# A streaming encoder layer on 8 cores: the running stream last, the residual added by an accumulating DMA, and weights that arrive in smaller pieces

## The chip, the cores and the metric

The kernel runs on the 8 NeuronCores of one Trainium2 chip. Each core computes one prompt stream of 2048 frames and two running streams of 16 frames; the cores exchange nothing. The metric is the device time in microseconds (us) of the slowest core.

## What is computed

```python
def _layer(x, pos, S_ret, S_hg, w_in, w_out, g_pre, g_post, lb):
    h = _rmsnorm(x, g_pre)
    u = jnp.einsum('btd,de->bte', h, w_in)
    cuts = np.cumsum([RET_WIDTH] * 4 + [HG_WIDTH] * 3)
    rq, rk, rv, rg, hq, hf, hi, hg = jnp.split(u, cuts.tolist(), axis=-1)
    ...
    hq = jax.nn.silu(_heads(hq, HG_HEADS))
    f = lb + (1.0 - lb) * jax.nn.sigmoid(_heads(hf, HG_HEADS))  # forget gate in (lb, 1)
    logf = jnp.log(f)
    hk = 1.0 - f
    hv = _heads(hi, HG_HEADS)
    o_r, o_h, S_ret, S_hg = _run_mixers(S_ret, S_hg, rq, rk, rv, hq, hk, hv, logf, log_gamma)
    o = jnp.concatenate([jax.nn.silu(rg) * _merge(_head_norm(o_r)), jax.nn.silu(hg) * _merge(_head_norm(o_h))], axis=-1)
    y = jnp.einsum('bte,ed->btd', o, w_out)
    return x + _rmsnorm(y, g_post), S_ret, S_hg
```

The model width is 1024; w_in is 1024 x 4096 and its columns are 8 segments of 512 (0 and 1: the retention's q and k; 2 and 3: its v and gate; 4 and 5: HGRN2's q and forget gate; 6 and 7: its v and gate). w_out is 1024 x 1024. Both recurrences have 4 heads of 128 and carry one 128 x 128 state per head. All inputs are fp32.

## The kernel before

A core's prompt is cut into 4 blocks of 512 frames, and each block into 4 tiles of 128 frames. Its two running streams are one more block, called the sample, with one tile of 48 rows. Every step is recorded once by `S.op(engine, function, reads, writes)`; afterwards `Sched.list_schedule` simulates the engines with a table of costs and writes the order of each engine out. That order is fixed in the program: each engine (PE, ACT, DVE, POOL, and SP, which only issues DMAs) works through its list and waits at an operation until its inputs are there. `add_fillers` puts small matmuls of the identity (L1047) into places where the simulation sees PE idle.

- `front(block)` runs `stage_A` for each tile: load x into `xs` (the first two odd ones into `xr`), sum of squares on ACT, power on POOL, scaling into `xbf` on DVE (L619), transposed into `xT` by PE in block 0 and the sample (L633) and by a transposing DMA elsewhere (L625). It then runs `stage_B_hg` for each head: two projections of the whole block (L654, segments 5 and 4), ACT, two scans on DVE, products on POOL (L721, L731).
- `tile(block, j)` runs `stage_B_ret` (segments 0 and 1, L671, rotary products on DVE, sums on POOL in L759, transposes), `stage_C` (segments 2, 6, 3, 7, L671), `stage_D` (scores L835, output L867 and L872, state update L884, head norms: ACT L895, POOL L899 and L902, DVE L905) and `stage_E`.
- `stage_E` transposes the gated output `og` into `ogT` (by DMA at L926, or by PE at L934 in block 0, in the sample and in the last tile), multiplies by `Wo` (two banks of 8 matmuls, L947), sums the squares on ACT (L951), multiplies the bank by `gpost` on DVE (L954), takes the power on POOL (L957, L959), and on DVE scales and adds x (L962). That x was loaded a second time into `xr` by SP (L923). SP stores `xr` to `yp` (L970). There are two `xr` buffers.

The weights are fp32 in HBM and bf16 in SBUF, so POOL issues their DMAs, which cast. Segments 0 and 1 (the first pair) come in four pieces of 2 x 128 rows, the other pairs and `Wo` in two pieces of 4 x 128 rows. Only the projections of segments 0 and 1 in block 0 are split into four groups of two matmuls, so that each group waits for its piece alone. A projection holds one of the 8 PSUM banks from its first matmul on, and `RESP` = 3 banks are kept free of projections when one is placed. In `front` and `tile` the program order is: blocks 0 to 2; block 3 with tiles 0 to 2; the sample; tile 3 of block 3.

## Time and profile before

| | |
|---|---|
| time, median of 3 runs | 387.5 us (386.18 to 388.3) |
| the profiled execution | 388.32 us, span of its slowest core 386.8 us |
| spans of the 8 cores in it | 381.1 to 386.8 us |
| PE, DVE, POOL, ACT busy | 93%, 66%, 53%, 47% of the span |

The span runs from the first to the last instruction of a core. The profiled execution took 1.5 us more than its slowest span. A matmul is pipelined: its busy time in a row holds some 0.16 us that the next one overlaps, so the step between the starts of two matmuls in a row tells more than the duration of one. Times in the rows are from the start of the span.

### The profile page before, as it was taken

The page shows a single profiled execution, that of the slowest core. Times are in us where ns is not written, and L with a number is a line of the kernel's source. Part 1 is how long each engine was busy: PE and PEld are TensorE (multiplying, and loading weights), DVE is VectorE, ACT ScalarE, POOL GpSimd, SP SyncE. Part 2 cuts the span into 40 slices and gives each one's busy share as a digit, 9 for nine tenths or more (in the row PEclk, how much of TensorE's full clock was granted, in tenths as well). Part 3 has the DMA queues.
Part 4 walks back from the last instruction along what each step waited for, and adds up shares of the span by engine and source line. Part 5 has one row for each costly group of instructions (what it writes and reads, how often), then busy time and mean ns, then how long its engine had stood idle before and what let it go on. Part 6 is the DMA issues. An engine that isn't in the chain of part 4 may idle for free.

```text
span 386.8 us, 8100 instructions; the slowest of 8 cores (381.1 to 386.8 us)
## 1 busy us (share of the span) xinstructions
PE 358.8 (93%) x2339; PEld 188.1 (49%) x2339; DVE 255.6 (66%) x554; ACT 180.9 (47%) x563; POOL 205.5 (53%) x277
## 2 busy tenths in 40 slices
PE   8599799998988989997999999999999999999982
PEld 8554354455544444453545454545455554554541
DVE  0316565827889998969395949386849467486364
ACT  2431245557767546471636253446262533646341
POOL 8525541545775785774283645375837436347130
PEclk9989899999999999998999999999999999999988
DMA  7999999996488476964537335432233443233217
GB/s 177 204 177 165 202 163 168 178 242 150 87 219 173 157 169 146 231 160 102 153 67 190 88 121 73 164 71 64 55 125 72 133 107 97 110 56 79 101 22 225
DMA packets 64700, 52.62 MB, mean 136 GB/s; under 512 B 45840, under 2 KB 53040, under 8 KB 64656
## 3 DMA queue, kind: packets, MB, share of 16 engines
q1 hardware_dynamic: 59344, 41.61, 42.4%
q0 software_dynamic: 5312, 10.49, 17.7%
q8 instruction: 20, 0.33, 0.4%
q14 instruction: 24, 0.20, 0.2%
HBM read 41.73 MB, written 10.09 MB: 134 GB/s over the span
## 4 chain that ended last, share of the span: by engine, by line
PE 78%; DVE 6%; DMA 5%; issue 3%; POOL 3%; ACT 2%; SPq 1%; DVEq 0%; ACTq 0%; POOLq 0%; another core or an unknown queue 0%
PE bank L671 42%; PE bank L947 14%; PE bank L654 12%; DMA xr<-xp 4%; PE bank L867 2%; PE bank L835 2%; DVE xbf L619 2%; PE bank L872 2%; PE bank L884 2%; POOL QTh L731 1%; DVE fG L713 1%; DVE fR L725 1%; PE bank L934 1%; DMA ogT<-og 1%; SPq L849 1%
## 5 line engine op out<-in xcount | busy, mean ns | idle before, releaser
L671 PE MATMUL bank<-Wi,xT 128*128 128x512 bf16 (+1 forms) x816 | 187.8, 382 | 0.7 <-DVE Sst L889 0.7
L671 PEld LDWEIGHTS bank<-Wi,xT 128*128 128x128 bf16 (+1 forms) x816 | 78.3, 99 | 88.1 <-issue 4.1
L947 PE MATMUL bank<-Wo,ogT 128*128 128x512 bf16 (+1 forms) x272 | 65.1, 391 | 3.6 <-DMA ogT<-og 2.0
L905 DVE SCALAR_TENSOR_TENSOR og<-bank,rsq,gate 128x128 bf16<-128x128 f32 (+1 forms) x136 | 38.6, 343 | 41.2 <-POOL rsq L902 18.3
L654 PE MATMUL bank<-xT,Wi 128*128 128x512 bf16 (+1 forms) x320 | 63.0, 342 | 2.1 <-POOL QTh L731 0.9
L654 PEld LDWEIGHTS bank<-xT,Wi 128*128 128x128 bf16 x320 | 26.9, 98 | 34.2 <-issue 6.9
L947 PEld LDWEIGHTS bank<-Wo,ogT 128*128 128x128 bf16 (+1 forms) x272 | 26.5, 100 | 34.7 <-issue 7.4
L824 POOL TENSOR_TENSOR Sst<-Sst,decS 128x512 f32<-128x512 f32 x30 | 32.9, 1105 | 16.5 <-DVE Sst L889 8.7
L895 ACT ACTIVATE og<-bank 128x128 bf16<-128x128 f32 (+1 forms) x136 | 35.4, 291 | 9.7 <-PE bank L867 6.2
L902 POOL TENSOR_TENSOR rsq<-ssq,mhalf 128x4 f32<-128x4 f32 (+1 forms) x34 | 35.4, 1042 | 5.2 <-POOL ssq L899 0.4
L828 ACT ACTIVATE Sb<-Sst 128x512 bf16<-128x512 f32 x30 | 19.0, 634 | 38.7 <-POOL Sst L824 21.3
L759 POOL TENSOR_TENSOR qtm<-tA,tB 128x512 bf16<-128x512 f32 (+1 forms) x17 | 21.6, 1270 | 25.2 <-DVE tB L750 24.2
L951 ACT ACTIVATE og<-bank 128x512 bf16<-128x512 f32 (+1 forms) x34 | 20.4, 601 | 30.4 <-PE bank L947 25.3
L731 POOL TENSOR_TENSOR QTh<-fQ,fR 128x512 bf16<-128x512 f32 (+1 forms) x20 | 23.0, 1151 | 21.4 <-ACT fQ L729 10.7
L721 POOL TENSOR_TENSOR KTh<-fG 128x512 bf16<-128x512 f32 (+1 forms) x20 | 18.5, 924 | 28.0 <-DVE fG L713 28.0
L794 ACT ACTIVATE gate<-bank 128x512 bf16<-128x512 f32 (+1 forms) x34 | 20.4, 600 | 27.5 <-PE bank L671 26.2
L713 DVE TENSOR_TENSOR_SCAN fG<-bank,zer 128x128 f32<-128x128 f32 (+1 forms) x72 | 23.1, 377 | 14.9 <-ACT bank L708 14.8
L895 ACT ACTIVATION_READ_ACCUMULATOR og<-bank 128x1 f32 (+1 forms) x136 | 30.4, 224 | 0.0
L619 DVE SCALAR_TENSOR_TENSOR xbf<-xs,rsx,gpre 128x1024 bf16<-128x1024 f32 (+1 forms) x15 | 21.9, 1472 | 11.8 <-POOL rsx L616 11.6
L725 DVE TENSOR_TENSOR_SCAN fR<-bank,inv,zer 128x128 f32<-128x128 f32 (+1 forms) x72 | 27.5, 439 | 2.8 <-DVE inv L717 1.1
L962 DVE SCALAR_TENSOR_TENSOR xr<-bank,rs,xr 128x512 f32<-128x512 f32 (+1 forms) x34 | 25.3, 744 | 5.8 <-POOL ssq L899 3.3
L843 DVE TENSOR_TENSOR AT<-bank,maskT 128x512 bf16<-128x512 f32 x32 | 20.9, 682 | 10.5 <-PE bank L835 10.4
(93 smaller groups left out, 450.8 us busy)
## 6 DMA issues: line engine op xcount, KB each, us to landing
xr<-xp SPq DMA_DIRECT2D x18, 512.0 KB, 4.3
yp<-xr SPq DMA_DIRECT2D x16, 512.0 KB, 2.9
xs<-xp SPq DMA_DIRECT2D x14, 512.0 KB, 5.5
Wi<-w_in POOLq DMA_DIRECT2D x6, 1024.0 KB, 48.5
Wi<-w_in POOLq DMA_DIRECT2D x4, 512.0 KB, 20.3
Wo<-w_out POOLq DMA_DIRECT2D x2, 1024.0 KB, 71.8
rot<-rot_p SPq DMA_DIRECT2D x16, 96.0 KB, 5.0
gpre<-g_pre SPq DMA_DIRECT2D x1, 512.0 KB, 6.7
```

What stands on the lines that cost most here:

```text
L619: S.op(DVE, lambda e: e.scalar_tensor_tensor(out=xbf[slot][0:L, :], in0=xbuf[0:L, :], scalar=rsx[0:L, sq:sq + 1], in1=gpre[0:L, :], op0=AL ...
L654: ins = e.matmul(pb(v)[:, 0:nt], lhsT=Wi[:, kc, col0:col0 + 128], rhs=k.xT[:, kc, 0:nt], start=(kc == 0), stop=(kc == 7))
L671: ins = e.matmul(pb(v)[0:L, :], lhsT=k.xT[:, kc, j * 128:j * 128 + L], rhs=Wi[:, kc, seg * 512:(seg + 1) * 512], start=(kc == 0), stop=(kc ...
L713: S.op(DVE, lambda e, c=c: e.tensor_tensor_scan(out=G[:, c, rsl(cl - 1, cl)], data0=pb(v)[:, rsl(c * st_ + cl - 1, cl)], data1=zer[:, 0:cl ...
L725: S.op(DVE, lambda e, c=c: e.tensor_tensor_scan(out=pack(R)[:, c, :], data0=pb(v)[:, c * st_:c * st_ + cl], data1=zer[:, 0:cl], initial=IV ...
L731: S.op(POOL, lambda e: e.tensor_tensor(out=tok(k.QT[:, h, :]), in0=pack(SQ), in1=pack(R), op=ALU.mult), reads=["fQ", ("fR", f)] + [("fR", ...
L824: S.op(POOL, lambda e, Sst=Sst, cc=cc, g=g, gsl=gsl: e.tensor_tensor(out=Sst[:, gsl].rearrange("p (h e) -> p h e", h=4), in0=Sst[:, gsl].r ...
L895: S.op(ACT, lambda e, q_=q_, h=h, vo=vo: e.activation(out=ogs[vs][0:L, h * 128:(h + 1) * 128], in_=pb(vo)[0:L, q_ * 128:(q_ + 1) * 128], f ...
L902: S.op(POOL, lambda e, gq=gq, g=g: e.tensor_tensor(out=rsq[vs][0:L, gq], in0=ssq[vs][0:L, gq], in1=mhalf[0:L, 0:4], op=ALU.pow), reads=[(" ...
L905: S.op(DVE, lambda e, q_=q_, h=h, vo=vo: e.scalar_tensor_tensor(out=ogs[vs][0:L, h * 128:(h + 1) * 128], in0=pb(vo)[0:L, q_ * 128:(q_ + 1) ...
L947: ins = e.matmul(pb(y)[0:L, :], lhsT=ogT[:, kc, 0:L], rhs=Wo[:, kc, n * 512:(n + 1) * 512], start=(kc == 0), stop=(kc == 7))
L962: S.op(DVE, lambda e, n=n: e.scalar_tensor_tensor(out=xr[slot][0:L, n * 512:(n + 1) * 512], in0=pb(ybk[n])[0:L, :], scalar=rs2[0:L, 0:1], ...
```

## The change

- The second pair of segments is also loaded in four pieces, and in block 0 every projection is now split: in four groups for the first two pairs, in two groups for the others (`PARTS`), for `proj_fm` too.
- `stage_E` of 15 prompt tiles no longer loads x ahead and no longer multiplies by `gpost` apart. DVE multiplies bank, scale and `gpost` in one operation into `xr`; then POOL issues a DMA that adds x from HBM onto `xr` in SBUF, and SP stores `xr` when that has landed. The last tile of block 3 and the sample keep the old form.
- All weight DMAs have priorities one above the other; the x loads of tiles 4 and 5 wait for the third pair's last piece (was: the fourth pair's), and the load of `gpost` waits for the fourth pair's last piece (was: the first scores).
- The sample comes behind tile 3 of block 3.
- The simulation's model of the DMA queues is new, and its priorities get a fixed small noise, so the order changes in many places all over the program.

```diff
-DMA_RATE = 300.0
-SW_RATE = 275.0
-HW_SHARED = 120.0
+DMA_RATE = 310.0
+DMA_RATE_0 = 230.0
+HW_SHARE = 0.45
...
+class Net:
+    def __init__(self):
+        self.t = 0.0
+        self.queues = ([], [])
+        self.coming = []
+
+    def issue(self, t, soft, nbytes, op):
+        self.coming.append([max(t, self.t), 0 if soft else 1, float(nbytes), op])
+        self.coming.sort(key=lambda x: x[0])
...
+            rate = DMA_RATE if self.t > 12000.0 else DMA_RATE_0
+            rates = [rate] if len(on) == 1 else [rate * (1.0 - HW_SHARE), rate * HW_SHARE]
...
-                if e == POOL:
-                    if o["nbytes"] > 600000:
-                        sw_free = max(fin, sw_free) + o["nbytes"] / SW_RATE
-                        dlat = (sw_free - fin) + o["lat"]
-                    else:
-                        dlat = 4500.0
-                else:
-                    share = 9000.0 < fin < sw_free
-                    hw_free = max(fin, hw_free) + o["nbytes"] / (HW_SHARED if share else DMA_RATE if o["lat"] > 1500.0 else 150.0)
-                    dlat = (hw_free - fin) + o["lat"] + (3000.0 if share else 0.0)
-                o["t_land"] = fin + dlat
-                o["t_dma"] = o["nbytes"]
+                net.issue(fin + (4500.0 if e == POOL else 0.0), e == POOL, o["nbytes"], i)
+                if e != POOL and o["nbytes"] < 120000 and len(net.queues[0]) > 1:
+                    o["lat"] += 3500.0
...
-        loads = [(w_in_v, Wi, "Wi", 0, 2), (w_in_v, Wi, "Wi", 1024, 4), (w_in_v, Wi, "Wi", 2048, 4), (w_in_v, Wi, "Wi", 3072, 4),
+        loads = [(w_in_v, Wi, "Wi", 0, 2), (w_in_v, Wi, "Wi", 1024, 2), (w_in_v, Wi, "Wi", 2048, 4), (w_in_v, Wi, "Wi", 3072, 4),
...
-                S.ops[wid]["boost"] = (14.0e6 if wb < 4 else 10.0e6) - 5e5 * wb
+                S.ops[wid]["boost"] = 14.0e6 - 4e5 * wb
...
                 elif i < 6:
-                    S.ops[xid]["deps"].add(S.last_w[("Wi", 7, 3)])
+                    S.ops[xid]["deps"].add(S.last_w[('Wi', 5, 3)])
...
+        PARTS = (4, 4, 2, 2)
...
-            S.op(PE, mm, reads=WK(seg) + [("xT", k.par, j) for j in range(k.ns)], writes=[v] + claim)
+            parts = PARTS[seg // 2] if (not k.sample and k.b == 0) else 1
+            for q in range(parts):
+                k0, k1 = q * 8 // parts, (q + 1) * 8 // parts
+
+                def mm(e, k0=k0, k1=k1):
+                    ins = None
+                    for kc in range(k0, k1):
+                        ins = e.matmul(pb(v)[:, 0:nt], lhsT=Wi[:, kc, col0:col0 + 128], rhs=k.xT[:, kc, 0:nt],
+                                       start=(kc == 0), stop=(kc == 7))
+                    return ins
+                S.op(PE, mm, reads=WK(seg, k0 // 2, k1 // 2) + [("xT", k.par, j) for j in range(k.ns)], writes=[v] + (claim if q == 0 else []))
...
-            parts = 4 if (not k.sample and k.b == 0 and seg < 2) else 1
+            parts = PARTS[seg // 2] if (not k.sample and k.b == 0) else 1
...
                     for did in late_dma:
-                        S.ops[did]["deps"].add(scid)
+                        S.ops[did]["deps"].add(S.last_w[("Wi", 7, 3)])
...
+            acc = not k.sample and not (k.b == 3 and j == 3)
...
-            else:
+            elif not acc:
...
-                S.op(DVE, lambda e, n=n, y=y: e.tensor_tensor(out=pb(y)[0:L, :], in0=pb(y)[0:L, :],
-                                                              in1=gpost[0:L, n * 512:(n + 1) * 512], op=ALU.mult),
-                     reads=[y, "gpost", ("ss2", n)], writes=[y])
+                if not acc:
+                    S.op(DVE, lambda e, n=n, y=y: e.tensor_tensor(out=pb(y)[0:L, :], in0=pb(y)[0:L, :],
+                                                                  in1=gpost[0:L, n * 512:(n + 1) * 512], op=ALU.mult),
+                         reads=[y, "gpost", ("ss2", n)], writes=[y])
             S.op(POOL, lambda e: e.tensor_scalar(out=rs2[0:L, :], in0=ss2[0:L, 0:1], scalar1=ss2[0:L, 1:2], scalar2=EPS,
                                                 op0=ALU.add, op1=ALU.add), reads=[("ss2", 0), ("ss2", 1)], writes=["rs2"])
             S.op(POOL, lambda e: e.tensor_tensor(out=rs2[0:L, :], in0=rs2[0:L, :], in1=mhalf[0:L, 0:1], op=ALU.pow),
                  reads=["rs2", "mhalf"], writes=["rs2"])
-            for n in range(2):
-                S.op(DVE, lambda e, n=n: e.scalar_tensor_tensor(out=xr[slot][0:L, n * 512:(n + 1) * 512], in0=pb(ybk[n])[0:L, :],
-                                                                scalar=rs2[0:L, 0:1], in1=xr[slot][0:L, n * 512:(n + 1) * 512],
-                                                                op0=ALU.mult, op1=ALU.add),
-                     reads=[ybk[n], "rs2", ("xr", slot)], writes=[("xr", slot)])
+            if acc:
+                for n in range(2):
+                    S.op(DVE, lambda e, n=n: e.scalar_tensor_tensor(out=xr[slot][0:L, n * 512:(n + 1) * 512], in0=pb(ybk[n])[0:L, :],
+                                                                    scalar=rs2[0:L, 0:1], in1=gpost[0:L, n * 512:(n + 1) * 512],
+                                                                    op0=ALU.mult, op1=ALU.mult),
+                         reads=[ybk[n], "rs2", "gpost"], writes=[("xr", slot) if n == 0 else ("xr1", slot)])
+                S.op(POOL, lambda e: e.dma_start(out=xr[slot][:], in_=xp[t0:t0 + 128, :], accum_op=ALU.add),
+                     reads=[("xr1", slot)], writes=[("xr", slot)], dma_key=("xacc", slot))
...
-                stores.append(S.op(SP, lambda e: e.dma_start(out=yp[t0:t0 + 128, :], in_=xr[slot][:]), reads=[("xr", slot)], dma_key=("st", slot)))
+                stores.append(S.op(SP, lambda e: e.dma_start(out=yp[t0:t0 + 128, :], in_=xr[slot][:]), reads=[("xr", slot), ("xr1", slot)], dma_key=("st", slot)))
...
             if b == 3:
-                for j in range(3):
+                for j in range(4):
+                    if j == 4:
+                        front(smp)
+                        tile(smp, 0)
                     tile(blocks[b], j)
-                front(smp)
-                tile(smp, 0)
-                tile(blocks[b], 3)
+                if 4 == 4:
+                    front(smp)
+                    tile(smp, 0)
...
+        S.jitter = (15, 500.0)
```

PE, the stretch in which block 0 goes from segments 0 and 1 to segments 2 and 3. L671 (L733 in the changed kernel) is a projection with `Wi`, L774 (L836) the transposes of rotated q and k, L835 (L897) the scores of a tile, L1047 a filler. Before:

```order
16 L774 MATMUL bank<-ident,qtm 128x128 x4
17 L774 MATMUL bank<-ident,Ktr 128x128 x4
18 L671 MATMUL bank<-Wi,xT 128x512 x6
19 L835 MATMUL bank<-QKr 128x128 x4
20 L671 MATMUL bank<-Wi,xT 128x512 x6
21 L774 MATMUL bank<-ident,qtm 128x128 x4
22 L774 MATMUL bank<-ident,Ktr 128x128 x4
23 L1047 MATMUL bank<-ident 128x128 x12
24 L774 MATMUL bank<-ident,qtm 128x128 x4
25 L774 MATMUL bank<-ident,Ktr 128x128 x4
26 L1047 MATMUL bank<-ident 128x128 x6
27 L671 MATMUL bank<-Wi,xT 128x512 x16
```

The changed kernel, the same place:

```order
10 L733 MATMUL bank<-Wi,xT 128x512 x40
11 L836 MATMUL bank<-ident,qtm 128x128 x4
12 L836 MATMUL bank<-ident,Ktr 128x128 x4
13 L733 MATMUL bank<-Wi,xT 128x512 x4
14 L897 MATMUL bank<-QKr 128x128 x4
15 L733 MATMUL bank<-Wi,xT 128x512 x4
16 L836 MATMUL bank<-ident,qtm 128x128 x4
17 L836 MATMUL bank<-ident,Ktr 128x128 x4
18 L733 MATMUL bank<-Wi,xT 128x512 x22
19 L836 MATMUL bank<-ident,qtm 128x128 x4
20 L836 MATMUL bank<-ident,Ktr 128x128 x4
21 L733 MATMUL bank<-Wi,xT 128x512 x6
```

Projections stand now where fillers stood, and between the transposes of the tiles there are 22 and more of them.

SP, the first part of the program, behind the loads of the first tiles. Before:

```order
9 L984 DMA rot<-rot_p 128x192 x3
10 L560 DMA gpost<-g_post 128x1024
11 L984 DMA rot<-rot_p 128x192 x2
12 L602 DMA xs<-xp 128x1024 x2
13 L923 DMA xr<-xp 128x1024 x2
14 L625 DMA_TRANSPOSE xT<-xbf 128x8x128
15 L602 DMA xs<-xp 128x1024
16 L625 DMA_TRANSPOSE xT<-xbf 128x8x128
17 L602 DMA xs<-xp 128x1024
```

The changed kernel:

```order
9 L1058 DMA rot<-rot_p 128x192 x5
10 L658 DMA xs<-xp 128x1024 x3
11 L681 DMA_TRANSPOSE xT<-xbf 128x8x128 x2
12 L658 DMA xs<-xp 128x1024
13 L616 DMA gpost<-g_post 128x1024
14 L681 DMA_TRANSPOSE xT<-xbf 128x8x128
15 L658 DMA xs<-xp 128x1024
16 L681 DMA_TRANSPOSE xT<-xbf 128x8x128
17 L658 DMA xs<-xp 128x1024
18 L1058 DMA rot<-rot_p 128x192
```

The loads and transposes of block 1's tiles stand ahead of `gpost`, and the loads of `xr` are gone from the queue.

PE, the end of the program. L867 and L872 are the output of a tile's heads, L884 (L946) the state updates, L934 (L998) the transposes of `og`, L947 (L1011) the product with `Wo`; operands of 48 or 16 belong to the sample. Before:

```order
469 L872 MATMUL bank<-Sb,QTh 128x128
470 L947 MATMUL bank<-Wo,ogT 48x512 x16
471 L857 MATMUL bank<-ident,KTh 48x128 x4
472 L884 MATMUL bank<-V,Ktr 128x128 x12
473 L934 MATMUL bank<-ident,og 128x128 x8
474 L884 MATMUL bank<-V,Kth 128x128 x8
475 L947 MATMUL bank<-Wo,ogT 128x512 x16
476 L884 MATMUL bank<-V,Kth 128x128 x4
```

The changed kernel:

```order
475 L934 MATMUL bank<-xbf,QTh 16x128 x2
476 L1011 MATMUL bank<-Wo,ogT 128x512 x16
477 L919 MATMUL bank<-ident,KTh 48x128 x4
478 L946 MATMUL bank<-V,Ktr 128x128 x8
479 L998 MATMUL bank<-ident,og 128x48 x8
480 L946 MATMUL bank<-V,Kth 128x128 x4
481 L1011 MATMUL bank<-Wo,ogT 48x512 x16
```

The sample's output product is last instead of the prompt's, and the prompt tile's stands behind the sample's last heads.

## Rows read from the trace of the kernel before

**Rows 1.** Cores: us from first to last instruction, granted TensorE clock.
```profile
core 7: 386.8 us, clock 0.980
```

**Rows 2.** Windows of core 7: us busy (instructions) of each engine, clock, DMA share, GB/s.
```profile
20.00:40.00 20.00, 19.35 (x132) 10.65 (x130) 9.39 (x24) 3.99 (x6) 6.93 (x8) 0.92 1.09 172
40.00:60.00 20.00, 17.66 (x118) 9.35 (x118) 10.66 (x22) 7.32 (x23) 9.43 (x10) 0.91 1.08 182
...
90.00:110.00 20.00, 18.13 (x132) 9.99 (x132) 16.88 (x30) 14.64 (x50) 13.95 (x20) 1.00 0.60 131
...
130.00:150.00 20.00, 18.82 (x105) 8.94 (x104) 18.29 (x33) 10.69 (x35) 14.36 (x17) 1.00 0.60 157
...
200.00:340.00 140.00, 139.43 (x844) 70.79 (x842) 96.19 (x215) 63.67 (x225) 74.89 (x98) 1.00 0.39 104
```

**Rows 3.** The chain of work that ended last, shares of the span by engine.
```profile
PE 78%; DVE 6%; DMA 5%; issue 3%; POOL 3%; ACT 2%; SPq 1%; DVEq 0%; ACTq 0%; POOLq 0%; another core or an unknown queue 0%
```

**Rows 4.** Timeline of PE: start, us, line, operation, count, idle before.
```profile
39.51 0.50 PE L1047 MATMUL bank<-ident 128*128 128x128 bf16 x6
...
43.43 5.30 PE L671 MATMUL bank<-Wi,xT 128*128 128x512 bf16 x16
...
59.79 5.34 PE L654 MATMUL bank<-xT,Wi 128*128 128x512 bf16 x24 [0.19 <-DMA Wi<-w_in]
...
92.25 3.62 PE L947 MATMUL bank<-Wo,ogT 128*128 128x512 bf16 x16
```

**Rows 5.** Weight DMAs on POOL: duration, first and last issue; time to landing.
```profile
L543 POOL DMA_DIRECT2D Wi<-w_in x2: 748/774/800, 4.4 to 5.1; - x2
DMA to landing us min/median/max: 24.8/28.0/31.2
...
L543 POOL DMA_DIRECT2D Wi<-w_in x2: 792/797/802, 5.8 to 6.5; - x2
DMA to landing us min/median/max: 37.1/41.6/46.1
...
L543 POOL DMA_DIRECT2D Wi<-w_in x1: 826/826/826, 8.8 to 8.8; - x1
DMA to landing us min/median/max: 50.9/50.9/50.9
...
L543 POOL DMA_DIRECT2D Wi<-w_in x2: 760/765/770, 9.6 to 10.3; - x2
DMA to landing us min/median/max: 56.3/58.9/61.6
...
L543 POOL DMA_DIRECT2D Wo<-w_out x2: 760/795/830, 12.9 to 13.7; - x2
DMA to landing us min/median/max: 66.5/71.8/77.1
```

**Rows 6.** Groups by line and form: count, busy us, mean ns, idle before.
```profile
L954 DVE TENSOR_TENSOR bank<-bank,gpost 128x512 f32<-128x512 f32 x32 | 21.8, 689 | 3.9 <-ACT og L951 3.9
```

**Rows 7.** DMA issues: count, KB each, median us from issue to landing.
```profile
xr<-xp SPq DMA_DIRECT2D x18, 512.0 KB, 4.3
yp<-xr SPq DMA_DIRECT2D x16, 512.0 KB, 2.9
```

**Rows 8.** Two loads at the start, under the weights' traffic.
```profile
xr<-xp SPq DMA_DIRECT2D x2, 512.0 KB, 14.2
```

**Rows 9.** Waits of PE from 90 to 180 us: total, times, longest.
```profile
PE bank L934 <- DVE og L905: 2.3, 3, 1.2
PE bank L947 <- DMA ogT<-og: 2.0, 1, 2.0
PE bank L835 <- POOL QTh L731: 0.9, 1, 0.9
```

**Rows 10.** Timeline of SP's queue and of PE around 172 us.
```profile
172.80 1.22 SPq L926 DMA_TRANSPOSE ogT<-og  x1
176.10 3.01 PE L947 MATMUL bank<-Wo,ogT 128*128 128x512 bf16 x8 [2.00 <-DMA ogT<-og]
```

**Rows 11.** Timeline of the last tile: PE, then SP's last store.
```profile
374.16 5.30 PE L947 MATMUL bank<-Wo,ogT 128*128 128x512 bf16 x16 [1.04 <-ACT ogT L937]
...
383.38 0.34 SPq L970 DMA_DIRECT2D yp<-xr  x1
```

More of the change, by code:

```diff
@@ L175, in list_schedule @@
             prio[i] += o.get("boost", 0.0)
+        if self.jitter is not None:
+            noise = np.random.RandomState(self.jitter[0]).uniform(-1.0, 1.0, n) * self.jitter[1]
+            for i in range(n):
+                prio[i] += float(noise[i])
         XLAT = 110.0
@@ L186, in list_schedule @@
                 avail[o["eng"]].append(i)
-        free_t = {e: 0.0 for e in ENGS}
-        sw_free, hw_free, cold = 11500.0, 0.0, 0.0
-        port_free = 0.0
+        free_t = {e: 900.0 for e in ENGS}
+        cold, port_free = 0.0, 0.0
+        net = Net()
         order = {e: [] for e in ENGS}
@@ L197, in free_bank, with landed @@
             return min(fr, key=lambda k: (free_at[k], k))
+        def landed(until):
+            out = net.advance(until)
+            for i, t in out:
+                o = ops[i]
+                t += o["lat"]
+                o["t_land"] = t
+                for sx in succ[i]:
+                    ready_t[sx] = max(ready_t[sx], t + XLAT)
+                    ndeps[sx] -= 1
+                    if ndeps[sx] == 0:
+                        avail[ops[sx]["eng"]].append(sx)
+            return len(out)
         while done < n:
@@ L227, in list_schedule @@
                     best = (e, cand[1], cand[2])
+            if landed(best[2] if best is not None else None):
+                continue
             if best is None:
@@ L280, in list_schedule @@
                     avail[ops[sx]["eng"]].append(sx)
-        self.est_makespan = max(free_t.values())
+        landed(1e9)
+        self.est_makespan = max(max(free_t.values()), max(o.get("t_land", 0.0) for o in ops))
         return order
```

53 lines of the change are left out of this document (43 added, 10 removed).

## The prediction

> **What bounds the kernel now.** I read the cores first: the slowest span is 386.8 us [rows 1]; the execution took 388.3 us, 1.5 more, and lies 0.8 above the median of the runs (387.5). Then the chain of work that ended last: PE holds 78% of it, no other engine over 6% [rows 3]. So the time is PE's work plus the places where PE doesn't get on. The windows say where those are [rows 2]. From 200 to 340 us PE is busy for 139.43 of 140 us at clock 1.00: there a freed engine buys nothing. The losses lie before, and in the last tile.
>
> PE's work can be priced by the step: 16 full-width matmuls take 3.62 us, and 0.16 of it overlaps the next, so 0.216 each; a 128-column one takes (0.50 - 0.16) / 6 = 0.056 [rows 4]. In the first 90 us PE is fed by the weight stream, with the DMA engines full (share 1.09 and 1.08 [rows 2]). Issue plus time to landing [rows 5]: the first pair is complete at 4.4 + 24.8 = 29.2 us, the second has its halves at 36.3 and 42.9, the third at 52.6 and 59.7, the fourth at 65.9 and 71.9, `Wo` at 79.4 and 90.8. PE has finished segments 0 and 1 by 39.5, plays fillers and waits, and begins segments 2 and 3 at 43.43, right behind the landing at 42.9. Those 16 matmuls take 5.30 us instead of 3.62: the granted clock fell during the wait (mean 0.91 of 2.4 GHz over that window, some of it at the 1.2 GHz level) [rows 2, 4]. At 59.79 PE again starts on a landing; `Wo` lands at 90.8 and is first used at 92.25 [rows 4].
>
> **The change, step by step: pieces and splits.** I counted in each kernel's PE order how much work stands ahead of the wait for each landing, and took it off the landing time. The result is how late PE would run, at the least, for that wait alone; the largest so far rules. Before: second pair 64 full and 60 small matmuls, 17.2 us of work, 42.9 - 17.2 = 25.7; third 120 and 100, 31.5, so 28.2; fourth 184 and 104, 45.5, so 26.4; `Wo` 240 and 156, 60.5, so 30.3. The real start at 92.25 gives 31.8: 1.5 of other waits on top.
>
> Changed, with the same landings: last piece of the second pair 82 and 60, 21.1 us, so 21.8; third pair, first half 104 and 88, 27.4, so 25.2, second half 134 and 100, 34.5, so 25.2; fourth, first half 176 and 104, 43.8, so 22.1, second half 200 and 108, 49.2, so 22.7; `Wo` 300 and 156, 73.5, so 17.3. The wait for `Wo` goes, since 60 more full-width matmuls, block 1's among them, stand ahead of it. What is late next is the third pair (25.2) and then perhaps the fourth, because the x loads now start when the third pair has landed. A 2 MB half piece landed 6.0 us behind the one before it (65.9 to 71.9), so two x loads of 0.5 MB cost some 3 us of stream and four cost 6: the fourth pair's 22.7 becomes 25.7 or 28.7. `gpost`, 0.5 MB, leaves the third pair's stretch and gives it 1.5 us. I take 25.7. Against 31.8 that is 6.1 us, and I leave the 1.5 us of other waits as they are: **-4.6 us**. Bounds: 0 (all given back at block 1's transposes) and -6.6 - 1.5 = -8.1 (25.2, no other waits).
>
> **DVE and the order of blocks 0 to 2.** 30 multiplications by `gpost` go: 0.689 us each [rows 6], 20.7 us of DVE. The operation that takes their place is of the same form as the scaling-and-adding that it replaces, so nothing is added. From 200 us on it's hidden by PE's own work. From 90 to 180 DVE is 84 to 91% busy in the two windows shown [rows 2] and PE waits: 2.3 us for `og` from DVE, 2.0 for `ogT`, 0.9 for `QTh`, and 2.4 in smaller ones not shown; the 8 matmuls behind the `ogT` wait then take 3.01 us instead of 8 x 0.216 + 0.16 = 1.89, and as much again is lost right after [rows 9, 10]. That is 7.6 us of waits and some 1.7 of slow clock. About 8 of the 30 multiplications fall in this stretch, 5.5 us. The new order will have waits of its own, so I take somewhat under half: **-4 us** (bounds 0 and -9).
>
> **The tail.** Before, the last tile is a prompt tile, and after its heads' output PE has too little to do: it waits 1.04 us for the last `ogT`, 0.6 for `og` ahead of that, and its last 16 matmuls take 5.30 us, 1.7 above 3.62 [rows 11]: 3.4 us in all. Now the prompt tile's product with `Wo`, 3.45 us, lies in the gap in which the sample's last heads are normed. The norm (four squares on ACT, power on POOL, four products on DVE, transposes, copy) takes some 4.5 us and PE has 4.3 us of work for it. What follows the last matmul is the same chain with 48 rows and two small stores in place of one. **-2 us** (bounds 0 and -3.4).
>
> **The accumulating DMA.** No row shows one. Its bytes are those of the `xr` load that it replaces, so the traffic stays. What changes is that it stands between DVE's last operation on a tile and the store, and the store stands in SP's in-order queue with the transposes for `QKr`, `Kth` and `ogT` behind it. Below, it takes what the plain load took, 4.3 us; above, what such a load took under full traffic, 14.2 [rows 7, 8]. I take 6, nearer to the plain one, since most of these come after the weights. The new order's simulation allows 4.5 + 2.0 + 0.5 MB / 310 KB per us = 8.2 us, so at 6 SP hardly waits at the store. An `xr` buffer then is taken for 6 + 2.9 us more, and its tile comes round only two tiles later, some 40 us. POOL issues 15 more DMAs at some 0.8 us [rows 5], 12 us over a span in which it is 53% busy; behind one of them stand head norms of the next tile, hidden by PE's backlog from 200 us on. **+1 us** for both (bounds 0 and +12: three or four stalls like the one at 172.80, of 2.0 us and the slow clock behind it).
> The Trainium skill ("DMA: Bandwidth & Descriptors", on the anatomy of a DMA issued by GpSimd) gives such a DMA 2.0 us + bytes / 436 KB per us, an estimated 3.2 us for 0.5 MB; it prices no addition, and by it the sum wouldn't move.
>
> **The sum.** 388.3 - 4.6 - 4 - 2 + 1 = 378.7 for an execution like the profiled one, and 377.9 against the median: 378.
>
> **Rivals.**
> (a) The lead is given back in block 0: four x loads and block 1's transposing DMAs go into the full stream, the fourth pair and `Wo` land 6 us later, and projections of block 1 wait for `xT`, whose last transposes stand behind `gpost` in SP's queue. For it: DMA share 1.08 then. Against it: `Wo` has 13 us to spare. Only 1 of the 4.6 us stays: 382. Chance 0.18.
> The same page of the Trainium skill (on issuing engines not being separate DMA queues) says that DMAs of all engines run on the same 16 DMA engines and interleave; the share near 1 agrees, and it speaks for this case.
> (b) Slower: the accumulating DMA takes over some 9 us, so SP stands at the store past its planned time and the transposes behind it come late for PE, tile after tile. At 12 us, 4 late each time, with about 4 to spare at most places, 1 to 2 us in ten tiles and a fall of the clock in a few: +14 in place of +1, 391. It decides from about 9 us on. For it: 14.2 us under traffic, and one late `ogT` cost nearly 4 us at 172.80. Against it: 4.3 us is the usual. Chance 0.13.
> (c) The waits from 90 to 180 go nearly all, and the tail's: 372.5. For it: DVE has 5 us less to do there. Chance 0.13.
> (d) Gains and new waits cancel, or the accumulate's added waits just match the lead: 387. Chance 0.06.
> My forecast has 0.50, with its own range of 375 to 381.5.
>
> **Range and chances.** Over 0.5% of 387.5, about 2 us, is what a measurement of this kernel can tell. Faster: 0.50 + 0.18 + 0.13 = 0.81, less a little for (a) coming out worse, 0.80. Within 0.5%: 0.07. Slower: 0.13. The range goes from 371.5, (c) with a margin, to 387, which holds (a) and leaves (b) out.
>
> **What would show it.** In the profile after: no fillers and no gap ahead of segments 2 and 3, and granted clock 1.00 from 40 to 60 us; the first product with `Wo` some 13 us of work further on in PE's order, at 99 to 101 us; DVE busy some 235 us; PE still full from 200 to 340; the last `Wo` product at full clock. The accumulate's time from issue to landing decides (b): near 6 us I'm right on it. I'd be wrong if PE waited for transposing DMAs more than 2 or 3 us in all, if the fourth pair landed after 76 us, or if new waits of DVE and POOL in blocks 0 and 1 ate the lead.

## The result: 2.2% slower

The changed kernel takes **396.9 us** (median of four executions, 395.99 to 410.74) against 387.9 for the kernel before, run beside it: a ratio of **1.022 [1.017, 1.028]**. Predicted were 378.0 us and a range of 371.5 to 387, so it is a miss by 18.9 us, on the other side of no change. In some executions of these kernels one die ran at a lower clock; they are left out of every ratio and time below.

The page of the profiled execution (396.8 us; core 6, span 395.2). The chain of work that ended last, by engine and by line:

```profile
PE 70%; DMA 12%; DVE 6%; issue 4%; POOL 4%; ACT 3%; POOLq 0%; DVEq 0%; ACTq 0%; SPq 0%
PE bank L733 39%; PE bank L1011 12%; PE bank L716 11%; DMA xT<-xbf 7%; DMA Wi<-w_in 5%; PE bank L929 2%; PE bank L934 2%; PE bank L946 2%; PE bank L897 2%; DVE tA L808 1%; DVE fG L775 1%; DVE AT L905 1%; DVE xbf L675 1%; ACT og L1015 1%; DVE fR L787 1%
```

PE had 78% of it before [rows 3]; DMA has gone from 5 to 12%, and 7% of the span are the transposing DMAs into `xT`, which the page before doesn't show among its largest rows. The windows of core 6 say where:

```profile
40.00:60.00 20.00, 19.59 (x124) 10.07 (x126) 10.83 (x22) 7.40 (x23) 9.43 (x10) 1.00 1.07 169
...
80.00:90.00 10.00, 3.35 (x16) 1.32 (x14) 0.00 (x0) 0.89 (x1) 0.00 (x0) 0.90 1.27 169
90.00:110.00 20.00, 17.11 (x102) 9.48 (x105) 13.76 (x21) 12.98 (x37) 12.61 (x16) 0.80 0.45 115
130.00:150.00 20.00, 19.03 (x106) 9.25 (x106) 13.97 (x30) 11.25 (x29) 15.62 (x19) 1.00 0.70 157
...
170.00:200.00 30.00, 25.66 (x132) 12.33 (x133) 20.35 (x44) 11.70 (x35) 17.95 (x20) 0.89 0.57 104
200.00:340.00 140.00, 138.91 (x835) 71.28 (x848) 90.31 (x200) 66.10 (x234) 84.82 (x107) 1.00 0.52 107
```

From 40 to 60 us it is as predicted: PE full, clock 1.00 where it was 0.91 [rows 2]. Then, from 80 to 90, DVE and POOL do nothing and PE is busy for 3.35 us, after which the granted clock is 0.80 on the mean over 20 us (PE runs partly at 1.2 GHz). A second, smaller loss lies from 170 to 200. From 200 to 340 nothing has changed. PE's two longest waits from 60 to 200 us (total, times, longest):

```profile
PE bank L897 <- POOL QTh L793: 9.4, 1, 9.4
PE bank L929 <- DVE AT L905: 4.2, 1, 4.2
```

**How late PE runs.** For a point in PE's order I take its start and subtract the priced work ahead of it (0.216 us a full-width matmul, 0.056 a 128-column one, as in the prediction; fillers count nothing). A step in this number is a loss, wherever it is waited for. Worked out from the starts of each profiled execution's slowest core (e4 and e5 are described below; the x gate is the weight piece that block 1's first two x loads wait for; 328 is the start of the last product with `Wo`):

```
us of work ahead     20    35    50    55    65    80   130   140   328
before             27.7  28.0  29.4  29.8  31.4  33.7  36.6  41.5  46.1
changed            23.6  24.2  31.0  43.2  43.3  44.0  53.0  53.1  56.2
x gate back (e5)   22.0  22.8  25.3  26.1  29.5  36.2  42.1  42.3  45.4
before + pieces    24.6  25.9  32.4  32.6  33.4  34.1  38.0  40.1  44.7
```

The changed kernel is 4.1 us ahead at 20 us of work and has lost that at 50. It loses 12.2 at one place between 50 and 55, and 7.0 at another just before 130 (170 us of the span), where the kernel before has a loss of 4.9 of its own a little later. From 140 to 328 it gains 1.5, and 1.7 more inside the last product, which took 5.30 us before [rows 11] and takes 3.61 now. That leaves 10.1 - 1.7 = 8.4 us, the difference of the two spans. The gate's row shows that e5 isn't free of loss either: between 55 and 80 it loses 10.1 us, where the changed kernel loses 0.8. What the gate is worth below is what is left of both.

### The profile page after: what moved, and what is told of

Its sections match the earlier page's. It is cut to its first block, busy times and chain, and to the rows that moved or that the text cites. A ratio compares the mean times of both kernels' runs of the same rounds, so it can differ in the third digit from the quotient of the medians.

```text
span 395.2 us, 7895 instructions; the slowest of 8 cores (388.8 to 395.2 us)
## 1 busy us (share of the span) xinstructions
PE 357.1 (90%) x2303; PEld 188.5 (48%) x2341; DVE 237.4 (60%) x524; ACT 181.1 (46%) x563; POOL 223.0 (56%) x294
## 4 chain that ended last, share of the span: by engine, by line
PE 70%; DMA 12%; DVE 6%; issue 4%; POOL 4%; ACT 3%; POOLq 0%; DVEq 0%; ACTq 0%; SPq 0%
PE bank L733 39%; PE bank L1011 12%; PE bank L716 11%; DMA xT<-xbf 7%; DMA Wi<-w_in 5%; PE bank L929 2%; PE bank L934 2%; PE bank L946 2%; PE bank L897 2%; DVE tA L808 1%; DVE fG L775 1%; DVE AT L905 1%; DVE xbf L675 1%; ACT og L1015 1%; DVE fR L787 1%
## 5 line engine op out<-in xcount | busy, mean ns | idle before, releaser
L733 PE MATMUL bank<-Wi,xT 128*128 128x512 bf16 (+1 forms) x796 | 190.8, 387 | 4.3 <-DMA Wi<-w_in 2.3
L733 PEld LDWEIGHTS bank<-Wi,xT 128*128 128x128 bf16 (+1 forms) x816 | 79.2, 100 | 92.7 <-issue 11.7
L716 PE MATMUL bank<-xT,Wi 128*128 128x512 bf16 (+1 forms) x312 | 61.0, 339 | 3.1 <-DVE fG L775 1.4
L1011 PE MATMUL bank<-Wo,ogT 128*128 128x512 bf16 (+1 forms) x262 | 61.3, 379 | 1.5 <-ACT og L957 0.9
L957 ACT ACTIVATE og<-bank 128x128 bf16<-128x128 f32 (+1 forms) x136 | 35.7, 283 | 12.5 <-PE bank L934 8.7
L886 POOL TENSOR_TENSOR Sst<-Sst,decS 128x512 f32<-128x512 f32 x30 | 31.3, 1050 | 17.7 <-DVE Sst L951 9.8
L1011 PEld LDWEIGHTS bank<-Wo,ogT 128*128 128x128 bf16 (+1 forms) x272 | 26.0, 98 | 30.0 <-issue 0.8
L821 POOL TENSOR_TENSOR qtm<-tA,tB 128x512 bf16<-128x512 f32 (+1 forms) x17 | 23.5, 1382 | 17.0 <-DVE tB L812 13.7
L890 ACT ACTIVATE Sb<-Sst 128x512 bf16<-128x512 f32 x30 | 19.0, 632 | 29.7 <-POOL Sst L886 18.4
L787 DVE TENSOR_TENSOR_SCAN fR<-bank,inv,zer 128x128 f32<-128x128 f32 (+1 forms) x72 | 28.2, 440 | 2.5 <-DVE inv L779 0.9
L957 ACT ACTIVATION_READ_ACCUMULATOR og<-bank 128x1 f32 (+1 forms) x136 | 29.2, 214 | 0.0
L951 DVE TENSOR_TENSOR Sst<-bank,Sst 128x512 f32<-128x512 f32 x30 | 20.1, 685 | 14.3 <-PE bank L946 11.3
L812 DVE TENSOR_TENSOR tB<-bank,rot 128x512 f32<-128x512 f32 (+1 forms) x34 | 22.9, 682 | 8.7 <-PE bank L733 6.7
```

Source lines behind the costliest of these rows:

```text
L716: ins = e.matmul(pb(v)[:, 0:nt], lhsT=Wi[:, kc, col0:col0 + 128], rhs=k.xT[:, kc, 0:nt], start=(kc == 0), stop=(kc == 7))
L733: ins = e.matmul(pb(v)[0:L, :], lhsT=k.xT[:, kc, j * 128:j * 128 + L], rhs=Wi[:, kc, seg * 512:(seg + 1) * 512], start=(kc == 0), stop=(kc ...
L787: S.op(DVE, lambda e, c=c: e.tensor_tensor_scan(out=pack(R)[:, c, :], data0=pb(v)[:, c * st_:c * st_ + cl], data1=zer[:, 0:cl], initial=IV ...
L821: S.op(POOL, lambda e, ts=ts, dst=dst: e.tensor_tensor(out=dst[0:L, :], in0=tA[ts][0:L, :], in1=tB[ts][0:L, :], op=ALU.add), reads=[("tA", ...
L886: S.op(POOL, lambda e, Sst=Sst, cc=cc, g=g, gsl=gsl: e.tensor_tensor(out=Sst[:, gsl].rearrange("p (h e) -> p h e", h=4), in0=Sst[:, gsl].r ...
L957: S.op(ACT, lambda e, q_=q_, h=h, vo=vo: e.activation(out=ogs[vs][0:L, h * 128:(h + 1) * 128], in_=pb(vo)[0:L, q_ * 128:(q_ + 1) * 128], f ...
```

## The stop at 80 to 93 us, row by row

SP's queue in the changed kernel, then who waited on core 6: ACT, POOL, DVE, PE (start, us, ..., idle time before and its releaser).

```profile
71.90 13.26 SPq L681 DMA_TRANSPOSE xT<-xbf  x2
85.32 0.47 SPq L658 DMA_DIRECT2D xs<-xp  x1
...
93.80 1.25 SPq L681 DMA_TRANSPOSE xT<-xbf  x1
```
```profile
89.11 1.06 ACT L666 ACTIVATE xbf<-xs 128x1024 bf16<-128x1024 f32 x1 [11.52 <-DMA xT<-xbf]
...
90.65 0.59 ACT L791 ACTIVATE fQ<-bank 128x512 f32<-128x512 f32 x1
...
91.38 1.26 POOL L793 TENSOR_TENSOR QTh<-fQ,fR 128x512 bf16<-128x512 f32 x1
...
91.47 2.25 DVE L675 SCALAR_TENSOR_TENSOR xbf<-xs,rsx,gpre 128x1024 bf16<-128x1024 f32 x1 [12.11 <-POOL rsx L672]
...
92.79 0.58 PE L897 MATMUL bank<-QTh,KTh 128*128 128x128 bf16 x4 [9.44 <-POOL QTh L793]
```

And the two transposing DMAs of 71.9 and 75.7 us: duration on the queue (min/median/max, ns) and time to landing.

```profile
L681 SPq DMA_TRANSPOSE xT<-xbf x2: 3516/6476/9437, 71.9 to 75.7; - x2
...
DMA to landing us min/median/max: 13.8/15.4/17.1
```

The first transposing DMA of block 1 goes out at 71.90, since its x load no longer waits for the fourth pair, and lands 17.07 us later (71.90 to 88.97). The same operation of the kernel before goes out at 89.6 and later, as the last weights land (90.8 [rows 5]):

```profile
L625 SPq DMA_TRANSPOSE xT<-xbf x6: 1217/1222/1332, 89.6 to 122.1; - x6
...
DMA to landing us min/median/max: 3.1/3.2/3.4
```

ACT's next operation is the sum of squares of the next tile (L666), which writes its squares into the same `xbf` buffer that the transposing DMA still reads. ACT works in order, so `fQ` of the heads' chain, whose projection PE had ended by 81 us, stands behind it, then POOL's `QTh`, then PE's scores. PE never waits for `xT` itself: it waits for block 0, because block 1's preparation stands ahead of it in ACT's queue.

The early gate costs time before the stop, too. The two x loads go out at 57.9 us, in the full stream, and land after 9.0 and 11.6; ACT reaches the first sum of squares before its x is there, and a head's `decS` and the next head's operations stand behind it:

```profile
67.04 1.06 ACT L666 ACTIVATE xbf<-xs 128x1024 bf16<-128x1024 f32 x1 [3.02 <-DMA xs<-xp]
```

From 35 to 50 us of work the changed kernel loses 6.8 us and e5 2.5. I take part of the difference to be this wait; no run isolates it.

## Experiments

"Orders kept" means that every engine's order is that of the parent kernel, with only the named instructions moved or gone; "made anew" that the scheduler placed everything again. Ratios are to the kernel before, run beside each, with 95% intervals; percentages below are differences of these ratios. e1, e2 and e8 have one execution each that counts, so no ratio: their differences are in us to the changed kernel's 396.9.

```
                                      us      ratio
e3  changed, no accumulating DMAs     390.9   1.006 [1.003, 1.010]
e4  before + pieces and splits        387.7   1.000 [0.997, 1.003]
e5  changed, x gate back              387.2   0.997 [0.995, 0.999]
e6  before + accumulating stage       394.2   1.018 [1.015, 1.021]
e7  before + sample last              389.0   1.004 [1.001, 1.007]
e9  e5 with plain residual load       392.8   1.013 [1.010, 1.016]
e10 changed, plain residual load      401.8   1.034 [1.030, 1.038]
e11 e6's orders, DMAs left out        391.7   1.010 [1.006, 1.014]
e12 before + pieces + sample last     388.3   1.001 [0.999, 1.004]
e13 e5, seed 16                       389.7   1.006 [1.003, 1.009]
e14 e5, seed 17                       403.0   1.040 [1.033, 1.046]
e15 e9, seed 16                       391.8   1.010 [1.003, 1.017]
e16 e9, seed 17                       395.8   1.021 [1.016, 1.026]
e17 changed, seed 16                  399.0   1.029 [1.024, 1.034]
e18 e6, store planned later           391.8   1.011 [1.008, 1.014]
```

**e1: is it `Wo`'s traffic?** Orders kept; the two `Wo` DMAs issued on POOL behind block 0's last `KTh`.

```
+            wo = [i for i in order[POOL] if ops[i]["dma_key"] is not None and ops[i]["dma_key"][0] == "Wo"]
...
+            order[POOL] = rest[:n_] + wo + rest[n_:]
```

> The changed kernel with every engine's order kept, except that POOL issues the two w_out DMAs behind the last KTh of block 0 (77.5 us in the changed kernel's trace) instead of at 10.9 and 12.7 us. Theory T (the transposing DMAs of block 1's first x tiles are slow because they share the 16 DMA engines with the weight stream, and ACT, DVE, POOL and PE stand behind their xbf buffer): they land within 4 to 8 us instead of 17.1 and 13.8, the 9.4 us wait of PE before 92.8 us is gone or under 3 us, and the time falls by 8 to 11 us to 386 to 389. Rival R1 (they are slow for a reason of their own, such as the queue of SP or the many x loads ahead): they still take over 12 us and the time stays at 396 to 397. Rival R2 (the accumulating DMAs cost the time): 396 to 397.

393.3 us, 3.6 below the changed kernel, less than I expected (386 to 389). The wait of 9.4 us is gone: with `Wo` out of the way, the two transposing DMAs at 70.9 and 74.8 us land in 5.0 and 3.1. But `Wo` is now issued at 77.5 and lands 12.5 and 18.4 us later, and the next two meet it. The third and the fourth transposing DMA of e1, core 0, each with its time to landing:

```profile
L685 SPq DMA_TRANSPOSE xT<-xbf x1: 1876/1876/1876, 81.6 to 81.6; - x1
...
DMA to landing us min/median/max: 15.6/15.6/15.6
...
L685 SPq DMA_TRANSPOSE xT<-xbf x1: 7357/7357/7357, 86.9 to 86.9; - x1
...
DMA to landing us min/median/max: 12.4/12.4/12.4
```

PE waits 5.2 us for `xT` itself now. The stall followed the weight stream: the same transposing DMAs land fast without `Wo`'s traffic and the next ones slowly with it.

**e2: is it the shared buffer?** Orders kept; more `xbf` buffers, so that the sum of squares of tiles 6 and 7 waits for no transposing DMA.

```
+                return 10 + i, xr[i % 2][:, 0:512].bitcast(BF16)
+            b = (i - 4) % 3 if i < 6 else (i - 8) % 3
+            return b, (xbf[0], xbf[1], xbx)[b]
```

> The changed kernel with every engine's order kept and more buffers for the scaled x tiles (xbf): tiles 6 and 7 use the still idle xr buffers, the later ones rotate over three. Nothing waits any more for a transposing DMA to have read its buffer, except three tiles later. Theory T: the transposes of tiles 4 and 5 remain slow (over 12 us), but ACT's sum of squares of tile 6 starts before 80 us, the wait of PE at 83 to 92.8 us shrinks to at most 3 us (xT is needed some 7 us later in PE's order), the event at 170 us (4.2 us, behind a transpose of 8.7 us) goes too, and the time falls by 8 to 14 us to 383 to 389. Rival R2 (accumulating DMAs): 396 to 397. A rival to T in which the slow transposes hold PE through xT itself and not through the buffer: PE waits as long, now at its first projection of block 1, and the time is over 393.

388.7 us, 8.1 below, within the range that I expected (383 to 389), but not by the way expected: PE's wait was to shrink to 3 us at most. SP's queue in e2, core 0, and PE's longest wait:

```profile
70.22 13.42 SPq L700 DMA_TRANSPOSE xT<-xbf  x2
83.80 0.47 SPq L676 DMA_DIRECT2D xs<-xp  x1
```
```profile
PE bank L949 <- ACT Sb L910: 7.5, 1, 7.5
```

The transposing DMAs are as slow as before, and hold SP for 13.4 us; the x load behind them is late, and ACT's sum of squares now waits for that. The stop is 7.5 us and comes later in PE's order. So the shared buffer is one link of the chain and not the whole of it: SP's queue carries the delay as well. By the measure of how late PE runs, e2 (core 0) still loses 11.3 us from 50 to 65 us of work, the changed kernel 12.3; but from 80 to 130 it loses 2.1 in place of 9.0, and about that on each of the four cores whose clock wasn't lowered. Most of what more buffers gain is gained at the second loss.

**e3: is it the accumulating DMA?** Orders kept, the 15 accumulating DMAs left out.

```
+            gone = {i for i, o in enumerate(ops) if o["dma_key"] is not None and o["dma_key"][0] == "xacc"}
...
+            order[POOL] = [i for i in order[POOL] if i not in gone]
```

> The changed kernel with every engine's order kept, without its 15 accumulating DMAs: x is not added to the output of 15 tiles, and SP stores a tile as soon as DVE has scaled it. Theory T: the 12 us at 83 to 93 us stay, since no accumulating DMA is issued before 120 us; the event at 170 us may shrink with the traffic; 393 to 397. Rival R2: SP stood at its stores for 22 us in all behind these DMAs and made transposes late for PE; then the time falls to 388 or below.

390.9 us, 6 less than the changed kernel; I had expected less from it. PE's wait for `QTh` stays, 9.2 us against 9.4, so it isn't the accumulate's. What goes is the second loss. At 151.95 us of the changed kernel an accumulating DMA (9.5 us to landing), an x load and a transposing DMA (8.7 us to landing) run together, and ACT waits again at the sum of squares:

```profile
153.68 3.29 SPq L681 DMA_TRANSPOSE xT<-xbf  x1
```
```profile
162.51 1.06 ACT L666 ACTIVATE xbf<-xs 128x1024 bf16<-128x1024 f32 x1 [5.95 <-DMA xT<-xbf]
```

PE's 4.2 us for `AT` at 170 us and the clock of 0.89 behind it follow. Without the DMAs PE loses 4.7 us from 80 to 130 us of work (e3, core 3) in place of 9.0.

**e8: both, e1 and e3.**

> The changed kernel, every order kept, with both edits of the earlier runs: w_out's DMAs issued behind the last KTh of block 0, and no accumulating DMAs (x is not added for 15 tiles). If the two causes are separate, their gains add: the late w_out gave 3 to 4 us (393.3 against 396.9), leaving the accumulates out gave 6 (390.4), so 386 to 388. If both act on the same waits, it is no better than 390.

387.8 us, as expected: 9.1 below the changed kernel, where e1 and e3 alone give 3.6 and 6. As far as one execution can tell, the two losses are separate and add up in one fixed order. PE still waits 5.0 us for `xT` here, as in e1.

**e5: the gate of the x loads, alone.** Order made anew.

```
-                    S.ops[xid]["deps"].add(S.last_w[('Wi', 5, 3)])
+                    S.ops[xid]["deps"].add(S.last_w[('Wi', 7, 3)])
```

> The changed kernel with one dependency as it was: the x loads of tiles 4 and 5 wait for the fourth pair's last weight piece again; the order is made anew with it. Theory T (transposing DMAs of block 1 beside the weight stream cost 7 to 12 us, whatever waits for them): with x loads at 74 us their transposes run behind or at the end of the w_out transfer, PE's idle time before 95 us falls from some 15 us to under 6, and the time falls by 6 to 11 us to 386 to 391, unless the first transposes still meet w_out (then 391 to 394). Rival (the wait belongs to the order and comes back in another form): 395 to 398.

387.2 us: one number in the source, with the order that follows from it, is worth **9.6 us**. Core 0's window and its transposing DMAs up to 105 us:

```profile
80.00:90.00 10.00, 7.55 (x70) 4.63 (x69) 7.30 (x16) 8.10 (x27) 8.42 (x10) 1.00 0.97 204
...
170.00:200.00 30.00, 30.00 (x182) 15.31 (x181) 21.14 (x49) 15.93 (x51) 19.31 (x25) 1.00 0.73 118
```
```profile
L681 SPq DMA_TRANSPOSE xT<-xbf x5: 1245/1727/2788, 82.4 to 104.3; - x5
...
DMA to landing us min/median/max: 3.6/4.6/8.4
```

The first goes out at 82.4 us in place of 71.9, with less of `Wo` left to land. In all seven profiled kernels with the early gate (the changed one, e1, e2, e3, e8, e10, e17) the slowest of these DMAs issued from 60 to 105 us takes 15.4 to 17.5 us to land; in those with the late gate it takes 3.2 to 5.1 (the old scheduler) and 8.1 to 11.3 (the new).

**e4, e7, e12: the parts in the kernel before,** its scheduler kept, order made anew.

```
-        loads = [(w_in_v, Wi, "Wi", 0, 2), (w_in_v, Wi, "Wi", 1024, 4), (w_in_v, Wi, "Wi", 2048, 4), (w_in_v, Wi, "Wi", 3072, 4),
+        loads = [(w_in_v, Wi, "Wi", 0, 2), (w_in_v, Wi, "Wi", 1024, 2), (w_in_v, Wi, "Wi", 2048, 4), (w_in_v, Wi, "Wi", 3072, 4),
...
-                for j in range(3):
+                for j in range(4):
```

> The kernel before, its own scheduler and DMA priorities, with the second weight pair in four pieces and the projections of block 0 split by PARTS, and nothing else of the change; the order is made anew. My prediction's step on pieces: PE goes on through 39 to 43 us without a wait and at full clock, a gain of 3 to 5 us in the first 60 us; the x loads still wait for the fourth pair, so the transposing DMAs of block 1 run behind the weights. 382 to 385 if the gain is kept, 386 to 389 if block 0's later waits take it back. By the rival view that splitting itself costs (held banks, more waits), over 389.

> The kernel before with the sample behind tile 3 of block 3, and nothing else; the order is made anew by its own scheduler. My prediction's step on the tail: 1 to 3 us less, 384.5 to 386.5, PE's last product with w_out at full clock. Rival (the sample's longer chain of small steps at the end gives back what the filled gap saves): 387 to 389.

> The kernel before with two parts of the change: the second pair in four pieces with split projections, and the sample last; scheduler, residual and x loads of before. Each alone came out within 0.4% of before. My theory, that the lead from the pieces is used up by the waits for the heads' chain in the third pair, says 386 to 389 here too. Rival, that the parts only pay together, as the sample's work fills other gaps: 383 to 385.

None gains: 387.7, 389.0 and 388.3 us. e7, the sample last and nothing else, is 0.1 to 0.7% slower, where I had expected 384.5 to 386.5. In e4 (pieces and splits) PE is 3.1 us ahead of the kernel before at 20 us of work and 2.1 at 35; at 40 it is 2.5 behind (30.7 against 28.2). The lead from the pieces is there, and it is gone within 5 us of work, ahead of any stop; PE's waits there (1.1, 1.2 and 0.7 us) are for the heads' chain of the tiles (DVE's scans, POOL's `QTh`), and the projections that could have covered it had been done already. That this cover is the reason I argue from the order; no run isolates it.

**e6, e11, e18: the accumulating stage in the kernel before.** e6 has the changed `stage_E` alone, made anew; e11 keeps e6's orders and leaves the 15 DMAs out; e18 is e6 with

```
-                        dlat = 4500.0
+                        dlat = 8500.0
```

in the old scheduler's latency of a small GpSimd DMA.

> The kernel before, its own scheduler and weight pieces, with the changed stage_E alone: 15 tiles get x by an accumulating DMA and lose the multiplication by gpost; the order is made anew. My prediction's step: DVE loses 20.7 us of work, PE's waits between 90 and 180 us shrink, 382 to 386. The view from the run without accumulating DMAs (they add traffic of longer stay, 5.5 to 9.5 us each, where transposing DMAs are waited for): no gain or a loss, 387 to 393.

> The kernel before with the accumulating stage, its orders on every engine kept, and the 15 accumulating DMAs themselves left out (so the residual isn't added in those tiles; the 7.5 MB of its loads are gone too). Theory A, that the DMAs themselves cost the 6 us (late stores, traffic beside the transposing DMAs): 386 to 389. Theory B, that the order which the scheduler makes with them is at fault, not the transfers: 393 to 395 as with them.

> The kernel before with the accumulating stage, and its scheduler told that a small DMA of GpSimd takes 8.5 us, not 4.5, so that it plans the store that stands in SP's queue later, as the changed kernel's scheduler does. If the 6 us come from SP standing at stores that are planned too early, this gives most of them back: 387 to 390. If they come from the transfers themselves or from POOL's added issues, it stays at 393 to 395.

e6 loses 1.8%, some 7 us, more than either view expected (382 to 386, 387 to 393). What SP stood waiting for, before (core 7), in e6 (core 4) and in e18 (core 3), one row of each (L400 is the line from which every wait is issued; the first row is stores waiting for DVE, the others stores waiting for the accumulating DMA):

```profile
SPq L400 <- DVE xr L962: 21.8, 12, 4.5
```
```profile
SPq L400 <- DMA xr<-xp: 54.9, 12, 8.1
```
```profile
SPq L400 <- DMA xr<-xp: 25.2, 5, 6.8
```

The DMA lands in 5.6 us (median), but a scheduler that plans 4.5 puts SP behind it for 55 us in all; planning it later halves that and gives back 0.7% (2.8 us). With the DMAs out and the order kept, 0.9% (3.3 us) come back. So the expectations for e11 (386 to 389, or 393 to 395) and e18 (387 to 390) both failed: e18 by 1.8 us, and e11, at 391.7, lies between its two theories: about half of e6's loss stays without the transfers and belongs to the order that it got.

**e9, e10, e13 to e17: how much is luck?** e9 and e10 use the plain residual load, order made anew; the others change the seed of the noise in the priorities.

```
-            acc = not k.sample and not (k.b == 3 and j == 3)
+            acc = False
...
-        S.jitter = (15, 500.0)
+        S.jitter = (16, 500.0)
```

> The changed kernel with block 1's x loads tied to the fourth weight pair again and with the old plain load of the residual, order made anew. It keeps the pieces, the splits, the sample last, the late `Wo` dependency and the new scheduler. If the two losses are what the runs so far say (12 us stop from the early x loads and transposes, some 6 us from the accumulating DMA), they add: 387.2 minus 4 to 6, so 381 to 384, faster than both kernels. Rival: the x load's gate accounts for all that there is to win, and what the accumulating DMA costs and saves balances once the order is made for it: 386 to 388.

> The changed kernel with the old plain load of the residual for all tiles, order made anew; the early x loads stay. My theory: the stop of 9.4 us at 83 to 93 us of the profile has nothing to do with the residual, so this stays slow, 389 to 392, as the run with the accumulating DMAs left out in the changed kernel's own order. Rival, that the accumulating DMA is what makes the change slow: 383 to 386.

> The changed kernel with block 1's x loads tied to the fourth weight pair, and the random part of the scheduler's priorities drawn with seed 16 for 15. With seed 15 it took 387.2. If the luck of an order is worth some 5 us, this and the one with seed 17 lie away from 387.2 and from each other, 387 to 395. If not, both lie within 1.5 us of 387.2.

> As the run before, with seed 17: 387 to 395 if an order's luck is worth some 5 us, within 1.5 us of 387.2 if not.

> The same with seed 16 and the plain load of the residual in place of the accumulating DMA; with seed 15 it took 392.8. If the accumulating DMA pays in the new order, this is some 5 us above the accumulating kernel with seed 16; if the difference at seed 15 was luck, it lies on either side of it.

> As the run before, with seed 17, to be set against the accumulating kernel with seed 17: 5 us above it if the accumulating DMA pays, on either side of it if seed 15 was luck.

> The changed kernel whole, with seed 16 for 15. The stop of 9 us comes from the early x loads and block 1's transposing DMAs in the full weight stream, which any seed has: 393 to 400. If it were a matter of this one order, 385 to 390.

```
                          seed 15   seed 16   seed 17
late gate, accumulate      387.2     389.7     403.0
late gate, plain load      392.8     391.8     395.8
early gate, accumulate     396.9     399.0       -
early gate, plain load     401.8       -         -
```

Down the columns, the early gate costs 9.6, 9.3 and (plain load) 9.0 us: much the same with two seeds and with both residuals. Seed 17 wasn't run with the early gate, and no run moves the gate with the orders kept. Plain load minus accumulate is +5.6, +2.1 and -7.2 with the late gate and +4.9 with the early one: no verdict. e10 was expected at 389 to 392 and took 401.8, though it has no accumulating DMA, as the plain load got an order of its own. Along the first row nothing differs but random numbers, and the times span 16 us (seed 17's is the mean of two executions). In e14 a like loss lies at another place. PE and ACT in e14, core 6:

```profile
126.12 0.27 PE L929 MATMUL bank<-V,AT 128*128 128x128 bf16 x1 [9.94 <-DVE AT L905]
```
```profile
117.76 1.06 ACT L666 ACTIVATE xbf<-xs 128x1024 bf16<-128x1024 f32 x1 [4.11 <-DMA xs<-xp]
```

A tile's sum of squares at the head of ACT's queue waits for a DMA, and the scans, `og` and `AT` stand behind it. I hoped that e9 (381 to 384 expected) would beat both kernels; it is slower than the one before. Of all that ran, only e5 comes out under it, by 0.3%.

## Why the prediction was wrong, by its own steps

- **Pieces and splits, "-4.6 us, bounds: 0 (all given back at block 1's transposes)": the step that failed.** The landings of the weights were right: the second pair complete at 42.2 us, the fourth at 74.3, `Wo` at 88.1, and PE was 4.1 us ahead at 20 us of work. But I counted only weights as what PE could be late for, and bounded the moved DMAs at nothing below zero. The moved gate put two transposing DMAs into the full stream; they took 17.1 and 13.8 us where I silently kept 3.2, and I hadn't followed what else writes their source buffer. The price of the gate, shown by e5 and twice more (e13 against e17, e9 against e10), is 9.0 to 9.6 us. The first product with `Wo` began at 117.22, not at 99 to 101. The lower bound of -8.1 was wrong in itself: 31.8 - 25.2 = 6.6 us holds the 1.5 of other waits already.
- **Rival (a)** named this place, the full stream and the transposing DMAs, and gave it 382 us. It looked for the wait at `xT` and let 3.6 us be given back; what came was one stop of 9.4 us and the slow clock behind it.
- "**I leave the 1.5 us of other waits as they are**" failed too. e4 shows the lead of 3 us gone between 35 and 40 us of work: ratio 1.000. So in the kernel before the term was 0 even with the gate where it was.
- **The accumulating DMA, +1.** The landing of 6 us was right (5.8 median in the changed kernel). Its price was not: in the changed kernel's fixed order the DMAs cost 6 us (e3), and as I read it the slow case, 9.5 us beside a transposing DMA and an x load, decides, not the median. Whether the stage as a whole costs or pays over many orders stays open: the four pairs have both signs. Rival (b), 391 with SP standing at the store, is near what e6 shows (394.2), though without its condition: the DMA lands in 5.6 us there, not in over 9. In the changed kernel SP waits only 22.1 us for these DMAs, and the loss comes by way of ACT. By the Trainium skill ("DMA: Bandwidth & Descriptors", on the anatomy of a DMA issued by GpSimd) the transfer would be an estimated 3.2 us; the runs measured 5.6 to 6.5 as medians, and the measurement decides.
- **DVE and the order, -4.** DVE is busy 237.4 us (235 foretold) and its relief bought nothing that shows: from 80 to 140 us of work the changed kernel loses 9.1 us, the one before 7.8, e5 6.1.
- **The tail, -2:** the size was right, its cause is not shown. From 140 us of work to the last product PE loses 3.1 us in place of 4.6, and the last product takes 3.61 us in place of 5.30, together 3.2 us, within the bounds. But e4, which keeps the prompt tile last, has its last product at full clock too (3.61 us), and e7, the new place alone, gained nothing. The last products of the changed kernel:

```profile
379.05 3.40 PE L1011 MATMUL bank<-Wo,ogT 128*128 128x512 bf16 x15 [0.16 <-issue]
...
384.23 3.61 PE L1011 MATMUL bank<-Wo,ogT 128*48 128x512 bf16 x16
```

- **What the forecast lacked altogether** is a spread for the order itself. The diff replaces the scheduler and adds random noise to its priorities; the kernel of e5 with three seeds spans 387 to 403 us. What the new scheduler itself is worth no run isolates. A sum of terms of 1 to 5 us can't be trusted to more than that, and a range of 371.5 to 387 gave no room for a bad order.

## What to carry to other kernels

When an edit lets a load go earlier, follow its chain to the end: the DMAs that it sets off run in the traffic of that moment, and each in-order queue in which they or their buffers' next writers stand (SP and ACT here) carries the delay into work that has nothing to do with them. Take the price of a DMA from a row under the same traffic, and where none exists, let the bound go past zero. Where a scheduler makes the order anew, time several seeds before a difference of a few per cent is put down to an edit; with orders kept, as in e3, a single edit can be priced to 1 or 2 us (e3's five executions lie between 389.6 and 391.6).
